# Passage to the second mixing section: other landing places from its fifth unit on, VectorE's splits and additions in another order

## What is computed

```python
x = x + jnp.concatenate([tok, mo], axis=-1) @ w_out[i]
u = rms_norm(x, g_mlp[i])
x = x + jnp.square(jax.nn.relu(u @ w_ff1[i])) @ w_ff2[i]     # end of layer 0
...
u = rms_norm(x, g_mix[i])                                     # start of layer 1
h = u @ w_in_moba[j]
tok = moba_mixer(h[..., :3 * TOK_WIDTH], ...)
mo = mem_cross_attention(h[..., 3 * TOK_WIDTH:], mem_n, ...)
```

## Time and profile before

| what | value |
|---|---|
| runs shown, us | 799.4, 801.11, 801.05 (median 801.05) |
| the profiled execution, us | 797.63 |
| its span, first to last instruction, us | 795.8 |
| mean granted TensorE clock | 0.998 of full |
| PE busy | 783.9 us (98%) |
| VectorE (DVE) busy | 615.7 us (77%) |
| ScalarE (ACT) busy | 463.2 us (58%) |
| GpSimd (POOL) busy | 115.7 us (15%) |
| chain that ended last, by engine | PE 93%, DVE 3%, DMA 2%, ACT 1%, issue 1% |

### The profile page before, as it was taken

The page is one execution under the profiler, slowest core; times in us unless marked ns, Lnnn a source line. Parts: engine busy times, 40 slices in busy tenths (PEclk is TensorE's granted clock), DMA queues, the critical chain, the costliest instruction groups (busy, mean ns, idle before and its releaser), DMA issues.

```text
span 795.8 us, 10769 instructions
## 1 busy us (share of the span) xinstructions
PE 783.9 (98%) x4114; PEld 652.7 (82%) x4114; DVE 615.7 (77%) x849; ACT 463.2 (58%) x657; POOL 115.7 (15%) x136
## 2 busy tenths in 40 slices
PE   8999999999999999999999999989999999999998
PEld 7998977778878778888888888767777888888886
DVE  6657997767686767589888897867865798888886
ACT  6646655654756554475655655547865655656651
POOL 0600300000130410060000000058920100000000
PEclk9999999999999999999999999999999999999999
DMA  9961453447656634645455556062336455555511
GB/s 344 359 194 40 159 194 124 141 155 289 223 182 215 208 106 153 271 158 212 168 203 208 173 201 212 1 219 98 107 106 262 161 212 212 193 182 207 200 65 53
DMA packets 51666, 142.69 MB, mean 179 GB/s; under 512 B 2928, under 2 KB 21504, under 8 KB 43296
## 3 DMA queue, kind: packets, MB, share of 16 engines
q1 hardware_dynamic: 49552, 135.08, 48.5%
q0 software_dynamic: 1776, 6.84, 2.4%
q10 hardware_dynamic: 288, 0.10, 0.0%
HBM read 140.95 MB, written 1.05 MB: 178 GB/s over the span
## 4 chain that ended last, share of the span: by engine, by line
PE 93%; DVE 3%; DMA 2%; ACT 1%; issue 1%; SPq 0%; ACTq 0%; DVEq 0%
PE bank L1876 38%; PE bank L2330 18%; PE bank L2283 13%; PE bank L2287 7%; PE bank L2050 2%; PE bank L2118 2%; PE bank L2252 2%; PE bank L1965 1%; PE bank L1932 1%; DMA raw<-in_w_in_moba 1%; PE bank L1899 1%; DVE w_lo L1231 1%; PE bank L2092 1%; PE bank L2018 1%; PE bank L2258 1%
## 5 line engine op out<-in xcount | busy, mean ns | idle before, releaser
L1876 PE MATMUL bank<-w_hi,a_both 128*128 128x512 f32 (+2 forms) x720 | 227.2, 385 | 2.1 <-DVE a_both L1243 2.0
L1231 DVE TENSOR_TENSOR w_lo<-raw,w_hi 128x2048 fp32r<-128x2048 f32 (+2 forms) x75 | 169.4, 2259 | 56.7 <-ACT w_hi L729 55.4
L729 ACT ACTIVATE w_hi<-raw 128x2048 fp32r<-128x2048 f32 (+2 forms) x75 | 141.1, 1881 | 41.4 <-PE bank L1876 12.1
L1876 PEld LDWEIGHTS bank<-w_hi,a_both 128*128 128x128 f32 x720 | 135.2, 189 | 24.8 <-issue 4.3
L2283 PE MATMUL bank<-a_both,w_hi 128*128 128x512 f32 x448 | 149.1, 395 | 0.0
L1876 PE MATMUL bank<-w_lo,a_both 128*128 128x512 f32 (+2 forms) x360 | 136.3, 379 | 0.0
L2287 PEld LDWEIGHTS bank<-a_both,w_lo 128*128 128x128 f32 x448 | 84.4, 188 | 16.7
L1231 DVE TENSOR_TENSOR w_lo<-m,w_hi 128x2048 fp32r<-128x2048 f32 (+2 forms) x36 | 79.6, 2210 | 21.1 <-ACT w_hi L729 19.0
L2287 PE MATMUL bank<-a_both,w_lo 128*128 128x256 f32 x448 | 88.7, 280 | 0.0
L1091 ACT ACTIVATE memkv<-bank 128x512 f32<-128x512 f32 x64 | 37.9, 595 | 80.8 <-PE bank L2283 80.2
L2283 PEld LDWEIGHTS bank<-a_both,w_hi 128*128 128x128 f32 x448 | 76.0, 188 | 4.3 <-ACT memkv L1091 0.2
(11 more groups left out here) (274 smaller groups left out, 1246.7 us busy)
## 6 DMA issues: line engine op xcount, KB each, us to landing
m<-in_w_ff SPq DMA_DIRECT2D x32, 1024.0 KB, 4.9
raw<-in_w_ff SPq DMA_DIRECT2D x32, 1024.0 KB, 4.9
raw<-in_w_merge SPq DMA_DIRECT2D x8, 1024.0 KB, 5.0
raw<-in_w_out SPq DMA_DIRECT2D x8, 1024.0 KB, 5.3
raw<-in_w_in_moba SPq DMA_DIRECT2D x16, 512.0 KB, 4.6
m<-in_w_in SPq DMA_DIRECT2D x6, 880.0 KB, 9.1
raw<-in_w_mem_kv SPq DMA_DIRECT2D x4, 1024.0 KB, 5.3
raw<-in_w_ple_gate SPq DMA_DIRECT2D x4, 1024.0 KB, 5.0
```

The lines of the kernel that those rows point to most:

```text
L729: act.activation(w_hi[:, slot, 0:n], landing[land][:, 0:n], ACT.Copy).then_inc(hi_ready, 1)
L1231: dve.tensor_tensor(w_lo[:, v % RING, 0:n], landing[land_slot(v)][:, 0:n], w_hi[:, v % RING, 0:n].bitcast(F32), ALU.subtract).then_inc(lo_ ...
L1876: ins = pe.matmul(banks[t][:, 0:n], xa[:, kt, ts], wa[:, slot, w], start=(first[t] if isinstance(first, tuple) else first) and k == 0 and ...
```

## The change

Two edits. `land_slot` gives units 87 to 96 the other of the two `raw` places: 87 goes to place 0 (it was 1), 88 to place 1 (it was 0), and so on to 96, which goes to place 1 (it was 0). From 97 on the places are as before. On VectorE the c = 1 part of the flush leaves the loop and becomes a call of a new function, made after group 0; the split of 84, which was the last line of `mlp`, comes after `add_half(1, 2, 5)`. For the second MLP the same call stands right behind `mlp`, and the removed `unit` had nothing to split there (unit 130 does not exist).

```diff
         def land_slot(u):
-            return u % (RAW_IN if u < U_MERGE or U_FF0 <= u < U_MOBA + 2 or u >= U_FF1 else RAW)
+            if U_MOBA + 2 <= u < U_FF1:
+                return (u + 1) % RAW
+            return u % (RAW_IN if u < U_MERGE or U_FF0 <= u else RAW)
...
+            def flush_columns(lay, c, parts):
+
+                for t in range(NT):
+                    xs = x[:, t, c * CB:c * CB + CB]
+                    ins = dve.scalar_tensor_tensor(xs, parts[t], stat[:, 3, 5 + 2 * lay, t:t + 1], xs, ALU.mult, ALU.add)
+                link(ins)
+
...
-                    for c, parts in enumerate(((flush_m1, flush_u3), (flush_w, flush_u2))):
-                        for t in range(NT):
-                            xs = x[:, t, c * CB:c * CB + CB]
-                            ins = dve.scalar_tensor_tensor(xs, parts[t], r2[t], xs, ALU.mult, ALU.add)
-                        link(ins)
-                        if c == 0:
-                            block_done(base + 4 * FF - 2)
-                            add_half(0, 0, 5 + 2 * lay)
+                    flush_columns(lay, 0, (flush_m1, flush_u3))
+                    block_done(base + 4 * FF - 2)
+                    add_half(0, 0, 5 + 2 * lay)
...
-                unit(base + 4 * FF - 2)
-
...
-            groups(G_MIX1, 0, a_hi, a_lo, GAIN_MIX + 8)
+            group(G_MIX1, a_hi, a_lo, 0, GAIN_MIX + 8)
+            flush_columns(0, 1, (flush_w, flush_u2))
+            group(G_MIX1 + 1, a_hi, a_lo, 2, GAIN_MIX + 8)
             block_done(U_MOBA0 - 1)
             add_half(1, 2, 5)
+            unit(U_MOBA0 - 2)
             groups(G_MIX1, 2, a_hi, a_lo, GAIN_MIX + 8)
...
             mlp(U_FF1, 1, G_MLP1, GAIN_MLP + 8)
+            flush_columns(1, 1, (flush_w, flush_u2))
```

More of the change, by code:

```diff
@@ L1728, in flush @@
                     dve.wait_ge(m1_copied, lay + 1)
-                    r2 = [stat[:, 3, 5 + 2 * lay, t:t + 1] for t in range(NT)]
                     link(dve.tensor_tensor(flush_u2, bank[6], flush_m1, ALU.add))
```

## The result

| | before | changed |
|---|---|---|
| median of the first comparison, us | 800.27 (799.4 to 801.11, 4 runs) | 792.34 (792.27 to 793.84, 4 runs) |
| second comparison, another session, us | 799.64 (797.67 to 801.11, 11 runs) | 793.05 (792.64 to 795.23, 6 runs) |
| profiled execution, us (span) | 797.63 (795.8) | 793.84 (792.0) |
| mean granted clock, profiled execution | 0.998 | 1.000 |

The ratio of the times is 0.9909 (95% interval 0.9891 to 0.9927) in the first comparison and 0.9924 (0.9907 to 0.994) in the second.

What follows compares the result with a forecast made beforehand. The prediction took PE as the bound, delayed in the passage from first MLP to second mixing section by a chain over VectorE and landings. −6.5 + 1.5 = −5.0 us, taken from the median 801.05, gave 796.05; range 793.8 to 798.6.

Steps and rivals of the forecast that it cites:

- part 1: VectorE's order, units 81 to 84: group 0 before split 84, so unit 83 starts 2.1 us earlier, at 505.15.
- The 2.1: Forecast advance in us of unit 83's start, 505.15 in place of 507.26; counted within the 6.5.
- The two covers: Slack at units 83 and 84: half 1 ready 0.7 us, low part of 84 2.0 us before PE wants them.
- part 2: Landing places of units 87 to 96: 87 loads earlier, two PE waits go, second logits 6.5 us earlier.
- the 0.78 and 1.97: PE waits in us, in unit 86 and before the first logits, between first MLP and second mixing section; forecast to go.
- the 6.5: Forecast advance in us of the second logits, 536.6 instead of 543.13, including the advance at unit 83.
- part 3: Price at the second MLP: load 97 waits for the low part of 96 instead of 95; 1.5 us lost.
- The rival of evenly shared loads: Second MLP: loads 97 to 100 share the engines, 97 lands 9.4 us later, kernel 4.4 slower, 805.4; chance 0.03.
- the new wait cools PE: Rival: the new 1.5 us wait at the second MLP lowers PE's clock; gain 3.6, time 797.4; chance 0.12.
- The 7.1: Most the passage to the second logits could give, in us, with no wait before those logits.

Runs made afterwards that it cites:

- e2_order: The changed kernel with the old landing places, so only VectorE's order differs from the kernel before; median 795.89 us, ratio 0.9961.
- e3_last_places: The changed kernel with landing places 0 and 1 exchanged for the second MLP too; median 790.86 us, ratio 0.9898.
- the second profile: The kernel before, unchanged, profiled once more; one run, 800.34 us, mean granted clock 0.996.
- the third profile: The kernel before, unchanged, profiled a third time; one run, 798.43 us, mean granted clock 1.000.
- e8: e3_last_places with ScalarE's squares of q1 moved behind the exponentials of step 14; median 790.35 us, ratio 0.9888.
- e10: The same kernel as e8, run again in one session with the changed kernel; median 789.9 us, ratio 0.9876.
- e5_busy_all: The kernel before with fourteen extra matmuls, results unused, filling all of PE's waits in the passage; median 797.93 us, ratio 0.9983.
- e1_places: The kernel before with only the landing places of units 87 to 96 changed, VectorE's order kept; median 795.62 us, ratio 0.9952.

## Why the prediction was wrong where it was

**Right: part 1.** Unit 83 follows 82 without a wait; e2_order gives 1.95 for 2.1. The 2.1 was the wait and a little more: 507.26 less the 1.96 of the earlier trace rows is 505.30, not 505.15; it did not enter the sum by itself. The two covers held: neither half 1 nor the low part of 84 was waited for.

**Right: part 2.** The load of 87 issued at 510.70 (forecast 509.6, with the passage a microsecond late), the 0.78 and 1.97 went, 0.97 was left before the second logits (forecast about 1.0), and the 6.5 is 6.5.

**Right: part 3.** The forecast 1.5 us measured 1.64 as a wait; e3_last_places gave 1.5 back in time (792.34 to 790.86, two sessions). The rival of evenly shared loads did not occur: 97 stood 5.0 us from issue (599.42) to ScalarE's start, where it had been 4.9.

**Wrong: the step from the profile to the median.** "The profiled execution took 797.63 (span 795.8), giving 792.6; the median shown, 801.05, is 3.4 above that, and the forecast is on the median …". The 792.6 is 0.3 from what was measured; the 3.4 carried over to the changed kernel, without a reason for it, made the miss. They were no constant. Over 54 timed runs of before in three sessions the median is 799.34 (797.47 to 802.89): 1.7 of the 3.4 was a small sample. The rest is largely the granted clock: the 23 of these runs with a mean clock of 0.993 to 0.997 have a median of 800.57, the others about 798.8, and the fastest, 797.47, is close to the profiled one's time. The mean clock does not place a run by itself: the 30 runs at 0.998 go from 797.47 to 800.01, and it does not tell whether a fall met work with slack. The profiled execution had its half clock on such work; the second profile, at 800.34, paid for it. Filling the waits took off 1.6 us (ratio 0.9983, interval 0.9975 to 0.9992) without making anything earlier. That removing them gives the same 1.6 is an inference: the changed kernel's mean clock was 1.000 in eight of ten timed runs. So the change is worth 4.85 by the waits and, as an estimate, about 1.6 by the clock; of the 799.34 − 792.34 = 7.0 this leaves some 0.5 that no run settles; the 6.6 of the second comparison, one session, leaves nothing to speak of. Landings that differ from one execution to the next, 0.66 us in the third profile, are one candidate.

**The term left out** is thus the clock after the waits of before. The rival "the new wait cools PE" looked at the clock on the wrong side of the account: I priced the fall that the change might add at 1.4, from rows in which the half clock cost the span nothing, and left the fall that it removes out of the sum. Something like the rival did occur: two of the ten timed runs of the changed kernel had a mean clock of 0.998 and took about 2.2 us longer than the others of their session, and none of the twelve runs of e3_last_places, e8 and e10, without the new wait, was below 0.999. That the clock fell behind the new wait in those two is not shown; no profile was taken of them. The Trainium skill, "TensorE: Matmul & The Clock Gate" (on what is actually happening), says that the throttled state is the default and that activity releases it. The first profile agrees: PE was busy without a gap from 535 to 539 while PEclk went from 0.50 to 0.80, and it was 1.00 from 539 to 541. e5_busy_all fits too: with PE's idle time filled by useless matmuls, PEclk was 1.00 in all stretches shown.

**The range** was drawn around the wrong centre: its lower end of 793.8 is about 801.05 less 7.1 (793.95), where 797.63 less 5.0 was as good a centre and was not taken in. The 7.1 itself does not follow from its terms: 528.5 plus 1.14 plus 5.44 is 535.08, which is 8.05 before 543.13, and the two profiles without a wait in the passage (e8_q1_later and e10_q1_again, which have two edits more) have 535.89 − 491.74 = 44.15 to the second logits, 7.56 less than before.

## What to carry to other kernels

When a profiled execution is faster than the median of its own program, ask what the others pay before carrying the difference over: here it was the clock behind waits of two microseconds, and a change that removes such waits can take that with them. A landing place is a wait in disguise: exchange two by parity and look at the far end of the stretch, where parity meets the next rule; here two more lines gave back 1.5 us. Work that a covered wait lets run slowly is free only as long as the slow stretch does not slide past the point where the cover ends.

## What the runs showed of the hardware that was not expected

The same program with nearly the same waits fell to half clock at different places in different executions: behind 534 in one, behind 542 in another, not at all in a third; and the wait of 1.95 at 505, harmless in three profiles of before, brought PEclk to 0.83 over ten microseconds in e1_places. The cost in the profiles of before moved between nothing and 3.1 us. And an engine given fourteen useless matmuls made the whole kernel faster by 0.17%. The landing of the same unit, 89, took 4.55, 4.63 and 5.04 us in the three profiles of before, and the second logits, which hang on it, moved with it.
